# Four filler products of TensorE at the entry of each of two expert layers

## The reference

```python
def hier_moe(x, w_rg, b_rg, w_re, b_re, w1, w3, w2):
    g_prob = softmax(xt @ w_rg + b_rg)            # 4 groups
    grp = argmax(g_prob)
    e_logits = (xt @ w_re + b_re)                 # 32 experts, 8 in each group
    e_logits = take_along_axis(e_logits, grp)     # the chosen group's 8
    top_v, top_i = lax.top_k(e_logits, 2)
    gate = softmax(top_v) * g_w
    ...
    def block(args):                              # the tokens of one expert
        hdn = silu(xb @ w1[e]) * (xb @ w3[e])     # 1024 -> 512
        return (hdn @ w2[e]) * w[:, None]         # 512 -> 1024
```

## Time and profile before

| | us |
|---|---|
| median of 3 runs | 2996.56 |
| lowest and highest | 2993.69, 2999.35 |
| profiled execution | 2994.94 |
| its span, first to last instruction | 2993.1 |
| TensorE busy (share of the span) | 2895.8 (97%) |
| VectorE busy | 2123.5 (71%) |
| ScalarE busy | 1604.9 (54%) |
| POOL busy | 358.4 (12%) |

### The profile page before, as it was taken

How to read it: one execution, slowest core, us unless ns; L and a number is a source line. 1 busy time by engine, 2 the same in 40 slices (tenths; PEclk the granted TensorE clock), 3 DMA queues, 4 the chain that set the end, 5 groups by cost and what they waited for, 6 DMA issues and landing times.

```text
span 2993.1 us, 38811 instructions
## 1 busy us (share of the span) xinstructions
PE 2895.8 (97%) x14261; PEld 2257.0 (75%) x14261; DVE 2123.5 (71%) x2376; ACT 1604.9 (54%) x1969; POOL 358.4 (12%) x273
## 2 busy tenths in 40 slices
PE   8999899999989999899999999999999999999998
PEld 7668776767768767677677668888888887888886
DVE  3485799999972467899999865674776648676762
ACT  3573588888853464788888743433222226522211
POOL 0000212222220002122222220100000000000000
PEclk9999899999999998999999999999999999999999
DMA  7303799999962125899999844301232223232222
GB/s 273 136 1 113 261 389 405 409 398 400 405 223 85 39 99 226 334 399 398 404 399 406 332 106 99 66 20 64 92 102 95 99 85 99 92 111 93 91 94 84
DMA packets 170900, 600.50 MB, mean 201 GB/s; under 512 B 21697, under 2 KB 71025, under 8 KB 121363
## 3 DMA queue, kind: packets, MB, share of 16 engines
q1 hardware_dynamic: 140432, 541.22, 48.5%
q0 software_dynamic: 19840, 52.60, 4.9%
q10 hardware_dynamic: 10499, 4.91, 0.6%
HBM read 574.15 MB, written 40.37 MB: 205 GB/s over the span
## 4 chain that ended last, share of the span: by engine, by line
PE 73%; DMA 11%; DVE 7%; ACT 5%; issue 3%; POOL 1%; DVEq 0%; SPq 0%; ACTq 0%; POOLq 0%
PE bank L2074 14%; PE bank L2076 14%; PE bank L2075 14%; DMA ring<-w_gate 6%; PE bank L2512 4%; PE bank L2509 4%; DMA ring<-w_up 3%; PE bank L2086 3%; PE bank L2794 2%; PE bank L2528 2%; PE bank L2081 2%; PE bank L2082 2%; PE bank L2138 1%; PE bank L2139 1%; ACT ring_rounded L1479 1%
## 5 line engine op out<-in xcount | busy, mean ns | idle before, releaser
L3601 DVE TENSOR_TENSOR ring_rounded<-ring,big_rounded 128x2048 fp32r<-128x2048 f32 x252 | 567.6, 2288 | 32.0 <-ACT big_rounded L1479 31.0
L1479 ACT ACTIVATE big_rounded<-ring 128x2048 fp32r<-128x2048 f32 x252 | 481.9, 1916 | 44.2 <-DMA ring<-w_up 33.2
L3096 DVE TENSOR_TENSOR ring_rounded<-ring,ring_rounded 128x2048 fp32r<-128x2048 f32 (+2 forms) x118 | 261.4, 2255 | 329.8 <-ACT ring_rounded L1221 329.4
L1221 ACT ACTIVATE ring_rounded<-ring 128x2048 fp32r<-128x2048 f32 (+2 forms) x124 | 226.5, 1876 | 369.3 <-DMA ring<-ffn_w_down 150.1
L3601 DVE TENSOR_TENSOR ring_rounded<-ring,ring_rounded 128x2048 fp32r<-128x2048 f32 x128 | 292.4, 2288 | 43.5 <-ACT ring_rounded L1479 43.1
L1479 ACT ACTIVATE ring_rounded<-ring 128x2048 fp32r<-128x2048 f32 x128 | 245.0, 1917 | 96.5 <-DMA ring<-w_gate 95.5
L2074 PE MATMUL bank<-XT_rounded,ring_rounded 128*128 128x512 f32 (+1 forms) x792 | 295.8, 374 | 0.4 <-DVE XH_rounded L3149 0.4
L2076 PE MATMUL bank<-XT_rounded,ring_rounded 128*128 128x512 f32 (+1 forms) x792 | 292.9, 370 | 0.0
L2075 PE MATMUL bank<-XH_rounded,ring_rounded 128*128 128x512 f32 (+1 forms) x792 | 292.9, 370 | 0.0
L2512 PE MATMUL bank<-ring_rounded,big_rounded 128*128 128x512 f32 x960 | 265.7, 399 | 7.4 <-DVE ring_rounded L3601 6.9
L2075 PE MATMUL bank<-ring_rounded,XH_rounded 128*64 128x512 f32 (+2 forms) x608 | 239.6, 394 | 0.0
(11 more groups left out here) (525 smaller groups left out, 5527.1 us busy)
## 6 DMA issues: line engine op xcount, KB each, us to landing
ring<-w_up SPq DMA_DIRECT2D x128, 1024.0 KB, 9.8
ring<-w_down SPq DMA_DIRECT2D x128, 1024.0 KB, 7.7
ring<-w_gate SPq DMA_DIRECT2D x128, 1024.0 KB, 7.9
ring<-ffn_w_up SPq DMA_DIRECT2D x44, 1024.0 KB, 7.0
ring<-ret_gdn_w_in SPq DMA_DIRECT2D x8, 2048.0 KB, 13.1
ring<-ffn_w_down SPq DMA_DIRECT2D x8, 2048.0 KB, 7.7
expert_rows<-lnp POOLq DMA_DIRECT2D x1, 12288.0 KB, 40.3
ring<-odd_w_qkv SPq DMA_DIRECT2D x6, 2048.0 KB, 8.1
```

Source lines behind the costliest of these rows:

```text
L1221: act.activation(one_pass(hi(c)[:, ks, :]), raw(c)[:, ks, :], ACT.Copy).then_inc(rounded[c.pair], 1)
L1479: act.activation(one_pass(expert_hi(j)), expert_raw(j), ACT.Copy).then_inc(signal("half_rounded").sem, 1)
L3096: dve.tensor_tensor(one_pass(w), w, parts(hi(c)[:, ks, :]), ALU.subtract).then_inc(split[c.pair], 1)
L3601: dve.tensor_tensor(one_pass(expert_raw(j)), expert_raw(j), parts(expert_hi(j)), ALU.subtract).then_inc(signal("half_split").sem, 1)
```

## The change

Four filler products are put into each expert layer's entry: two between the last logits and `positions(l, 0)`, and two between `first_rows(l, 0)` and `positions(l, 1)`. They go into bank 4 in layer 0 and bank 6 in layer 1, at the use that stands next in the count, and leave the count as it is: the next user of the bank overwrites what they wrote. The loop over the halves is written out. Nothing else differs.

```diff
                 logits(l, 2)
                 logits(l, 3)
-                for q in range(2):
-                    positions(l, q)
-                    first_rows(l, q)
+                spare = (4, 6)[l]
+                keep_warm(Use(spare, U[f"moe{l}"][spare]), 2)
+                positions(l, 0)
+                first_rows(l, 0)
+                keep_warm(Use(spare, U[f"moe{l}"][spare]), 2)
+                positions(l, 1)
+                first_rows(l, 1)
```

## The result

| | before | after |
|---|---|---|
| median of 8 runs, us | 2994.65 | 3003.18 |
| lowest and highest | 2992.48, 2999.35 | 3000.06, 3006.98 |
| ratio, 95% interval | | 1.0026 (1.0016 to 1.0037) |
| span of the profiled execution | 2993.1 | 2999.5 |

The account below looks back on a forecast made before the run. TensorE was taken to bound the kernel (73% of the span). Layer 0's -4.48 - 1.75 = -6.23 and layer 1's -4.48 - 1.55 = -6.03 gave -12.3 us, from 2996.56 to 2984.3 us, range 2978 to 2998.

Parts of the forecast that it names:

- Price of a one-hot product at full clock: One-hot products of both halves: 0.12 us a record, taken from a wide expert's row turn, against 0.237 at half clock.
- nothing gained: Upper bound for a one-hot record at full clock: 0.237 us, as at half clock; the other bound was 0.118.
- At the same half clock in both, as their equal length shows: One-hot products before the change: 7.78 us in each half, read as both halves running at half clock.
- Does the clock hold? That is the whole forecast.: Layer entry: the forecast of 2984.3 us depends on the clock staying at 1.00 with the fillers; chance 0.58.
- rival 1: Clock drops as before or sooner, both pairs cost time: +4.64 us per layer, 3005.9 us in all; chance 0.12.
- Rivals 2 and 3: Clock lost at second pause: near 2995.3 us, chance 0.12; lost before up products or gain partly taken back: 2987.6 to 2991, 0.18.
- the forecast's picture of the fall: Layer entry: the clock drops after pauses among narrow products; a gap of over a microsecond may end either way.
- Pair 1, +1.22 us: Fillers behind the logits: 1.71 us at full clock, 0.49 hidden in idle time, so the first positions move by +1.22.
- Pair 2 "nearly free": Fillers between the halves: 1.71 us fit in the 2.15 us TensorE would idle waiting for VectorE's choice.
- Up products, -1.75 and -1.55: Expert 0's up products at full clock: gain of 1.75 us in layer 0, 1.55 in layer 1, some 1.0 hidden.
- The gather, "just enough": Expert 1's rows, layer 0: gather moves 1.3 us sooner, lands at 322.7 to 324.9 us, wanted at 324.9.
- I see no fixed appointment behind it; the shift should reach the end.: Behind the entry: weights are asked for by TensorE's progress, so the whole gain should reach the kernel's end.

Follow-up runs that it names:

- gapfill: Kernel before plus one filler product in each pause between positions and one-hot products, no other fillers: ratio 0.9994 (0.9983 to 1.0004).
- pair1: Kernel before plus only the two filler products between the last logits and the first half's positions, in each layer: ratio 1.0007 (0.9998 to 1.0016).
- contig_rows: contig with SP holding back the second half of expert 1's gate weights until expert 1's rows have landed: ratio 0.9964 against the kernel before.
- contig: Kernel before, no fillers, one-hot products loading 128 neighbouring columns, expert 0's gate and up weights read in matching order: ratio 0.9996 (0.9987 to 1.0004).
- contig_rows0: contig_rows with SP waiting for the rows before the first half of expert 1's gate weights too: ratio 0.9985 against the kernel before.
- second: Kernel before, no fillers, one-hot products loading every second column, expert 0's gate and up weights read in matching order: one execution, 2991.7 us.

## Why the prediction was wrong, point by point

- **Price of a one-hot product at full clock, the step that failed.** "I take 0.12, the row it is like": it measured 0.237 at either clock, the upper of the two bounds ("nothing gained"). 3.76 us per half, 15 us in all, hung on it. With 0.237 put into the forecast's own sum and the rest left as it was, layer 0 gets 1.22 + 1.71 - 0.35 - 1.75 = +0.83 and layer 1 +1.03 (an estimate from its terms). That is 14.1 of the 20.8 us between -12.3 and +8.5. The rest is the clock that wasn't held: about 4.4 in the pairs and 2.4 in the up products. The row turn looked alike in load pattern and columns, but it is a transpose of one record with 96 stationary partitions, and the one-hot product is a plain float32 product of two with 128. Which of these differences counts is open. That these two load a strided operand at so different a pace could be measured, not read off. A nearest row gives a bound; I used it as a value, while the other bound had the same right to it. "At the same half clock in both, as their equal length shows" is the same mistake: in the kernel after the halves are of equal length at unequal clocks.
- **"Does the clock hold? That is the whole forecast."** It wasn't. The clock did not hold, which is rival 1, but even where it was at 1.00 nothing was gained. Rivals 2 and 3 priced a held clock at a gain, and none had "the clock is held and makes no difference". Nor was the forecast's picture of the fall right: it looked at pauses, while the fall came inside unbroken one-hot products (after; `gapfill`) and within the logits (after, layer 1; `pair1`, layer 0).
- **Pair 1, +1.22 us.** 5.29 - 4.15 = 1.14 where the clock was up, as said; 6.97 - 4.16 = 2.81 in layer 1 where it had fallen during the logits. The range left that out.
- **Pair 2 "nearly free".** 2.80 us in layer 0 (309.80 - 307.00), 3.47 in layer 1, less 0.46 and 0.14 in faster positions. It was to lie in a wait for VectorE that exists only if the first half is fast. Rival 1 had its 3.42, and so came near: 3005.9 against 3003.18. Part of that is luck: it has 4.64 in each layer, and measured are 3.40 and 5.14, and pair 2 did lift the clock.
- **Up products, -1.75 and -1.55.** Theirs is the part that follows the clock: with the dense one-hot products before them, `contig_rows` needs 325.61 - 312.48 = 13.13 us against 13.80, wait for the rows included, and 12.2 in layer 1 against 13.61. VectorE's split does stand in the way: TensorE waits 0.86 us for it (`contig_rows`, 318.18). In the kernel after, layer 0 gained nothing and layer 1 0.90.
- **The gather, "just enough".** This step named the right place. With a fast entry (`contig`, layer 0) the rows were 4.7 us late, and what it missed is that the weights, moved forward with TensorE, would go out around the gather.
- **"I see no fixed appointment behind it; the shift should reach the end."** Wrong by half where the weights stay behind: `contig_rows0` has 11.3 us less in the entries and 4.5 less at the end. With the weights moved too, `contig_rows` keeps 10.8 of 12.0.
- The Trainium skill, "TensorE: Matmul & The Clock Gate", "LDWEIGHTS (loading the stationary operand)", prices a load by its columns alone. By the Trainium skill's figure a load of 128 columns is estimated at 107 ns. That is near the dense record at full clock (0.112 us) and the one of every second column (0.118), and not near the one of every fourth (0.233) or the dense one at half clock (0.213). The measurement decides. The Trainium skill, "TensorE: Matmul & The Clock Gate", "Part 4: PE-mode transpose", weighed in rival 1, would by that rival's reading have the turns lower the clock. The trace doesn't agree here: in the kernel after the clock was at 1.00 from 286.0 to 292.6 us, with 8 turns at a time between logits. Turns alone for longer are in no run.

Open: what decides whether the clock falls during the logits. It stayed up in layer 0 and fell in layer 1 of the same execution, with the same instructions. And `contig`'s shorter entries (5.8 us) left 1.2 by the ratio, not to be told from none; layer 0's part went in the stage behind the row turn, as shown, and what happened to layer 1's was not traced.

## What to carry to other kernels

Before a product is to be sped up by TensorE's clock, find rows of the same product at both levels; if there are none, the bound "nothing gained" is a case with a chance of its own and not an end of the range. A pace that was the same at both clocks pointed to the load of the stationary operand here, and the layout of that operand, with the order of the weights and one wait of SP that go with it, was worth more than any filler (10.8 us against a loss). When an entry gets shorter, look at which transfers now start at the same time, and give way to the small one that is needed first.

## What the runs showed of the hardware

A plain float32 product with 96 moving columns takes 0.233 us a record from start to start (0.237 with the start of a half) if its 128 stationary columns lie 16 bytes apart, at 2.4 GHz as at 1.2 GHz (`after`, `gapfill`). With 8 bytes it takes 0.118 us (`second`) and with neighbouring ones 0.112 (`contig`) at 2.4 GHz, and 0.213 at 1.2 in both. Transposes with the same 16 bytes take 0.12 us at 2.4 GHz. The clock may rise and fall within one unbroken run of the same product (0.50, 1.00, 0.50 within 7.58 us, `gapfill`). After a wait of 4.69 us it stood at 0.50 through the next 13 wide products (`contig`). A gather issued between two weight loads of 1 MB took 11.3 us to land (`contig`), against 4.7 to 6.9 before.
